# Two wide projections in the retention stage, with small elementwise work moved from GpSimd to ScalarE and VectorE

## The reference, cut to what matters

```python
def odd_mixer(xn, pos, w_in, ...):
    h = jnp.einsum('bsd,de->bse', xn, w_in)
    cx, dq, dk, dv, z = jnp.split(h, splits, axis=-1)
    oc = rglru_branch(cx, ...)              # stage C
    od = head_group_norm(retention_chunked(heads(dq), heads(dk), heads(dv), pos), ...)   # stage D
    y = jnp.concatenate([oc, od], axis=-1) * jax.nn.silu(z)
    return jnp.einsum('bse,ed->bsd', y, w_out)
# in rglru_branch, with xf the convolved input:
    r, ig = sigmoid(xb @ wa + ba), sigmoid(xb @ wx + bx)
    log_a = -RG_C * r * softplus(-lam)
    a = exp(log_a); u = sqrt(-expm1(2.0 * log_a)) * ig * xf
    h = scan(h_t = a_t * h_{t-1} + u_t)
# in retention_chunked: rotary(q), rotary(k) over the whole head, masked scores, values
```

## Time and profile before

| what | value |
| --- | --- |
| median of 3 runs | 579.88 us (579.59 to 580.05) |
| the profiled execution | 579.21 us, of which 577.5 us from the first to the last instruction |
| mean granted TensorE clock | 0.997 of 2.4 GHz |
| busy: PE | 569.6 us (99%) |
| busy: DVE | 440.1 us (76%) |
| busy: ACT | 398.5 us (69%) |
| busy: POOL | 67.8 us (12%) |

### The profile page before, as it was taken

How to read it: one execution, slowest core, us unless ns; L and a number is a source line. 1 busy time by engine, 2 the same in 40 slices (tenths; PEclk the granted TensorE clock), 3 DMA queues, 4 the chain that set the end, 5 groups by cost and what they waited for, 6 DMA issues and landing times.

```text
span 577.5 us, 8748 instructions
## 1 busy us (share of the span) xinstructions
PE 569.6 (99%) x3312; PEld 501.1 (87%) x3312; DVE 440.1 (76%) x696; ACT 398.5 (69%) x612; POOL 67.8 (12%) x76
## 2 busy tenths in 40 slices
PE   8999999999999999999999999999999999999995
PEld 7898889888888888888888889999899988888984
DVE  7888599698848874568768886799998974876763
ACT  7677794686657575647767858979669738466764
POOL 4002006039001000100000001111110100100002
PEclk9999999999999999999999999999999999999998
DMA  8757456457943544564346455326444564356202
GB/s 292 233 179 228 157 166 205 161 163 202 288 151 115 177 146 147 201 225 156 146 146 194 171 185 209 119 87 247 177 145 147 201 233 134 106 204 231 96 1 74
DMA packets 53134, 98.83 MB, mean 171 GB/s; under 512 B 1860, under 2 KB 8548, under 8 KB 53092
## 3 DMA queue, kind: packets, MB, share of 16 engines
q1 hardware_dynamic: 51908, 96.95, 49.9%
q0 software_dynamic: 1024, 1.05, 0.8%
q10 hardware_dynamic: 160, 0.27, 0.1%
HBM read 96.16 MB, written 1.05 MB: 168 GB/s over the span
## 4 chain that ended last, share of the span: by engine, by line
PE 97%; DMA 1%; DVE 1%; ACT 0%; issue 0%; DVEq 0%; SPq 0%; ACTq 0%
PE proj L2111 20%; PE proj L2112 10%; PE proj L2135 10%; PE proj L2137 10%; PE proj L2136 10%; PE proj L2094 5%; PE proj L2096 5%; PE proj L2095 5%; PE head L2341 4%; PE proj L2116 3%; PE proj L2115 1%; PE proj L2243 1%; PE head L2195 1%; DMA x_residual<-in_x_dram 1%; PE proj L2251 1%; PE head L2318 1%
## 5 line engine op out<-in xcount | busy, mean ns | idle before, releaser
L1258 DVE TENSOR_TENSOR w_lo<-raw_weights,w_hi 128x1024 fp32r<-128x1024 f32 x174 | 221.5, 1286 | 75.5 <-ACT w_hi L570 72.0
L570 ACT ACTIVATE w_hi<-raw_weights 128x1024 fp32r<-128x1024 f32 x174 | 181.9, 1056 | 99.6 <-PE proj L2137 48.2
L2111 PE MATMUL proj<-xT,w_hi 128*128 128x512 f32 x448 | 161.7, 400 | 0.0
L2112 PE MATMUL proj<-xT,w_lo 128*128 128x256 f32 x448 | 125.5, 280 | 0.0
L2111 PEld LDWEIGHTS proj<-xT,w_hi 128*128 128x128 f32 x448 | 84.3, 188 | 17.6
L2112 PEld LDWEIGHTS proj<-xT,w_lo 128*128 128x128 f32 x448 | 84.6, 189 | 2.0
L2094 PE MATMUL proj<-xT,w_hi 128*128 128x256 f32 x256 | 73.2, 286 | 0.0
L2095 PE MATMUL proj<-xT,w_hi 128*128 128x256 f32 x256 | 72.4, 283 | 0.0
L2096 PE MATMUL proj<-xT,w_lo 128*128 128x256 f32 x256 | 72.4, 283 | 0.0
L2135 PE MATMUL proj<-w_hi,y 128*128 128x512 f32 x176 | 69.2, 393 | 0.0
L2137 PE MATMUL proj<-w_lo,y 128*128 128x512 f32 x176 | 68.6, 390 | 0.0
(11 more groups left out here) (334 smaller groups left out, 937.7 us busy)
## 6 DMA issues: line engine op xcount, KB each, us to landing
raw_weights<-in_ev_w_in_dram SPq DMA_DIRECT2D x13, 2048.0 KB, 8.8
raw_weights<-in_od_w_in_dram SPq DMA_DIRECT2D x12, 2048.0 KB, 7.9
raw_weights<-in_ev_w_out_dram SPq DMA_DIRECT2D x4, 2048.0 KB, 7.9
raw_weights<-in_xa_wkv_dram SPq DMA_DIRECT2D x4, 2048.0 KB, 7.6
raw_weights<-in_od_w_out_dram SPq DMA_DIRECT2D x4, 2048.0 KB, 7.8
raw_weights<-in_xa_wq_dram SPq DMA_DIRECT2D x2, 2048.0 KB, 9.2
raw_weights<-in_xa_wo_dram SPq DMA_DIRECT2D x2, 2048.0 KB, 7.9
raw_weights<-in_ev_w_in_dram SPq DMA_DIRECT2D x6, 512.0 KB, 7.6
```

The lines of the kernel that those rows point to most:

```text
L570: act.activation(ring_quarter(w_hi, n, q), raw_quarter(n, q), ACT.Copy).then_inc(hi_ready, 1)
L1258: dve.tensor_tensor(ring_quarter(w_lo, n, q), raw_quarter(n, q), ring_quarter(w_hi, n, q).bitcast(F32), ALU.subtract).then_inc(lo_ready, 1)
L2111: pe.matmul(both, wh[:, k, :], x[:, :, k, :], start=(k == 0), stop=False)
L2112: pe.matmul(dst[:, 0:S], wl[:, k, :], x[:, 0, k, :], start=False, stop=False)
```

## The change

The q and k slabs of stage D group 0 become kind "X". Each half then needs a copy (ScalarE, `half_copied`) and a sum (VectorE, `half_summed`), after which the pair is free; the swap and the rotation read the sum in SBUF in place of PSUM. Both decay squares and `conv_high` go from GpSimd to ScalarE. The low part of the first gated scan goes from stage D group 0 to group 1 on VectorE, and one `y_low` goes from GpSimd to VectorE.

```diff
-    SLABS += [("D", "q", "F", _g), ("D", "k", "F", _g), ("D", "v", "T", _g), ("D", "z", "X", _g)]
+    SLABS += [("D", "q", "XF"[_g], _g), ("D", "k", "XF"[_g], _g), ("D", "v", "T", _g), ("D", "z", "X", _g)]
@@ gpsimd
-            decay_square(0)
             gated_input(1)
-            conv_high()
-            decay_square(1)
-            for i in range(5, 8):
-                y_low(i)
+            y_low(5)
+            y_low(7)
@@ scalar
             def tanhs(g):
...
-                last.then_inc(decay_ready, 1)
+                act.drain().then_inc(decay_ready, 1)
+            def decay_square(g):
+                act.wait_ge(input_gated, g + 1)
+                act.activation(conv_out(g), blocks(5), ACT.Square).then_inc(a_squared, 1)
+            def conv_high():
+                act.wait_ge(y_ready, 5)
+                act.activation(y_hi[:, 0:4, :], y_src(4), ACT.Copy).then_inc(conv_hi_ready, 1)
@@ scalar, stage_c: after z_half(z, 0)
                 if g:
+                    decay_square(0)
                     root_c(0)
+            def half_copied(n, w, u):
+                if n in D_WIDE:
+                    filled(act, n, 1, u)
+                    act.activation(blocks(w)[:, 2 * u:2 * u + 2, :], bank_halves(n, u, 0), ACT.Copy).then_inc(d_copied, 1)
@@ scalar, swap_halves: wide slabs wait for d_summed and read blocks(w)
@@ scalar, stage_d
+                half_copied(q, 0, 0)
                 ahead(q, 2)
-                swap_halves(q, 0)
+                swap_halves(q, 0, 0)
                 ahead(q, 3)
+                half_copied(q, 0, 1)
                 ahead(k, 0)
-                swap_halves(q, 1)
+                swap_halves(q, 0, 1)
...
                 if g == 0:
                     decays(1)
+                half_copied(k, 1, 0)
                 ahead(k, 2)
...
+                else:
+                    decay_square(1)
+                half_copied(k, 1, 1)
                 ahead(v, 0)
...
                 ahead(z, 0)
+                if g == 0:
+                    conv_high()
@@ vector
+            def gated_low(i):
+                G = i % 4
+                dve.wait_ge(y_hi_ready, i + 2)
+                dve.wait_ge(y_lo_ready, i + 2)
+                dve.tensor_tensor(y_lo[:, 4 * G:4 * G + 4, :], y_src(i), y_hi[:, 4 * G:4 * G + 4, :].bitcast(F32),
+                                  ALU.subtract).then_inc(y_lo_ready, 1)
+            def half_summed(n, w, u):
+                if n in D_WIDE:
+                    dve.wait_ge(d_copied, 2 * D_WIDE.index(n) + u + 1)
+                    rows = blocks(w)[:, 2 * u:2 * u + 2, :]
+                    dve.tensor_tensor(rows, bank_halves(n, u, 1), rows, ALU.add).then_inc(d_summed, 1)
+                    halves_freed(n, u)
@@ vector, stage_d
                 ahead(q, 0)
                 sum_z(slab("D", "z", 0) if g else slab("C", "z", 1), 1)
+                if g:
+                    dve.wait_ge(conv_hi_ready, 1)
+                    dve.tensor_tensor(y_lo[:, 0:4, :], y_src(4), ...)      # stood behind rope_full(q, 0) for g == 0
                 ahead(q, 1)
                 if g:
+                    dve.drain()
                     gated_d(0)
+                half_summed(q, 0, 0)
                 ahead(q, 2)
                 rope_full(q, 0, 0, q_ready, 4 * g + 1)
+                half_summed(q, 0, 1)
                 ahead(q, 3)
                 ahead(k, 0)
+                if g:
+                    gated_low(6)
                 ahead(k, 1)
+                half_summed(k, 1, 0)
                 rope_full(q, 1, 0, q_ready, 4 * g + 2)
...
                     one_minus_a2(1)
+                half_summed(k, 1, 1)
                 ahead(v, 0)
@@ tensor, stage_d: slab_x in place of slab_f for the wide slabs
```

More of the change, by code:

```diff
@@ L68 @@
 Z_SLABS = [n for n, s in enumerate(SLABS) if s[1] == "z"]
+D_WIDE = [n for n, s in enumerate(SLABS) if s[0] == "D" and s[1] in "qk" and s[2] == "X"]
 def slab(stage, part, g=0):
@@ L169, in hybrid_trunk @@
         a_squared = sem("a_squared")
+        input_gated = sem("input_gated")
         mem_landed = sem("mem_landed")
@@ L275, in hybrid_trunk @@
         halves_swapped = sem("halves_swapped")
+        d_copied = sem("d_half_copied")
+        d_summed = sem("d_summed")
         early_ms = sem("early_ms")
@@ L503, in gated_input @@
                 pool.wait_ge(igate_ready, g + 1)
[L504 to L515, removed]
+                pool.tensor_tensor(blocks(4), blocks(4), conv_out(g), ALU.mult).then_inc(input_gated, 1)
             def mem_placed(t):
@@ L1061, in tanhs @@
                 for h in range(4):
-                    last = act.activation(blocks(3)[:, h, :], blocks(3)[:, h, :], ACT.Tanh,
-                                          scale=soft[:, 6, 4 * g + h:4 * g + h + 1])
-                last.then_inc(decay_ready, 1)
+                    act.activation(blocks(3)[:, h, :], blocks(3)[:, h, :], ACT.Tanh,
+                                   scale=soft[:, 6, 4 * g + h:4 * g + h + 1])
+                act.drain().then_inc(decay_ready, 1)
[5 more added lines that the diff above has]
+                act.activation(y_hi[:, 0:4, :], y_src(4), ACT.Copy).then_inc(conv_hi_ready, 1)
             def root_c(g):
@@ L1140, in rstd_d, with swap_halves @@
                 act.activation(wview(4), wview(4), ACT.Exp, scale=-0.5).then_inc(o_rstd, 1)
-            def swap_halves(n, u):
-                filled(act, n, u)
+            def half_copied(n, w, u):
+                if n in D_WIDE:
+                    filled(act, n, 1, u)
+                    act.activation(blocks(w)[:, 2 * u:2 * u + 2, :], bank_halves(n, u, 0), ACT.Copy).then_inc(d_copied, 1)
+            def swap_halves(n, w, u):
+                wide = n in D_WIDE
+                if wide:
+                    act.wait_ge(d_summed, 2 * D_WIDE.index(n) + u + 1)
+                else:
+                    filled(act, n, u)
                 for a, b in ((0, 64), (64, 0)):
-                    last = act.activation(rope_tmp[a:a + 64, 2 * u:2 * u + 2, :],
-                                          bank(n, u)[b:b + 64, :].rearrange("p (h t) -> p h t", h=2), ACT.Copy)
+                    src = (blocks(w)[b:b + 64, 2 * u:2 * u + 2, :] if wide else
+                           bank(n, u)[b:b + 64, :].rearrange("p (h t) -> p h t", h=2))
+                    last = act.activation(rope_tmp[a:a + 64, 2 * u:2 * u + 2, :], src, ACT.Copy)
                 last.then_inc(halves_swapped, 1)
@@ L1172, in stage_d @@
                     decays(1)
+                half_copied(k, 1, 0)
                 ahead(k, 2)
                 act.wait_ge(q_ready, 2 + 2 * g + 1)
-                swap_halves(k, 0)
+                swap_halves(k, 1, 0)
                 if g == 0:
@@ L1181, in stage_d @@
                     dm(1, 1)
+                else:
+                    decay_square(1)
+                half_copied(k, 1, 1)
                 ahead(v, 0)
                 act.wait_ge(q_ready, 2 + 2 * g + 2)
-                swap_halves(k, 1)
+                swap_halves(k, 1, 1)
                 ahead(v, 1)
@@ L1936, in stage_c @@
                     gated_c(0)
+            def gated_low(i):
[10 more added lines that the diff above has]
+                    halves_freed(n, u)
             def rope_full(n, u, w, done, i):
+                wide = n in D_WIDE
                 dve.wait_ge(halves_swapped, i)
-                src = bank(n, u)[:].rearrange("p (h t) -> p h t", h=2)
                 dst = blocks(w)[:, 2 * u:2 * u + 2, :]
+                src = dst if wide else bank(n, u)[:].rearrange("p (h t) -> p h t", h=2)
                 tmp = rope_tmp[:, 2 * u:2 * u + 2, :]
@@ L1945, in rope_full @@
                 dve.tensor_tensor(tmp, tmp, trig[:, 1:2, :].broadcast_to([P, 2, S]), ALU.mult)
-                dve.drain().then_inc(free_of(n, u), 1)
+                if wide:
+                    dve.drain()
+                else:
+                    dve.drain().then_inc(free_of(n, u), 1)
                 dve.tensor_tensor(dst, dst, tmp, ALU.add).then_inc(done, 1)
@@ L1987, in stage_d @@
                 sum_z(slab("D", "z", 0) if g else slab("C", "z", 1), 1)
-                ahead(q, 1)
                 if g:
[L1990 to L1993, removed]
                     dve.wait_ge(conv_hi_ready, 1)
@@ L1996, in stage_d @@
                                       ).then_inc(y_lo_ready, 1)
+                ahead(q, 1)
+                if g:
+                    dve.drain()
+                    gated_d(0)
+                half_summed(q, 0, 0)
+                ahead(q, 2)
+                rope_full(q, 0, 0, q_ready, 4 * g + 1)
+                half_summed(q, 0, 1)
                 ahead(q, 3)
                 ahead(k, 0)
+                if g:
+                    gated_low(6)
                 ahead(k, 1)
+                half_summed(k, 1, 0)
                 rope_full(q, 1, 0, q_ready, 4 * g + 2)
@@ L2565, in stage_d @@
                 q, k, v, z = (slab("D", c, g) for c in "qkvz")
-                slab_f(q, [0])
```

(6 more changed lines are left out.)

## The result

The changed kernel takes 581.15 us (median of 9 runs, 580.54 to 583.25) against 579.52 us of the kernel before, measured beside it (9 runs): 1.0029 times, 95% interval 1.0018 to 1.0040. That is 1.6 us slower, more than the 0.2% that counted as no change, though the lower end of the interval (0.18%) lies just inside it. The range of 579.0 to 581.9 holds the time. The forecast of 580.5 is 0.65 us short of it, and the forecast change of +0.64 us is 1.0 us short of the measured one: the kernel before, too, was faster here (579.52) than ahead of the prediction (579.88). The profiled execution has a span of 579.0 us against 577.5, which is 1.5 us more. One of the nine runs took 583.25 us at a mean granted clock of 0.995, the others 580.54 to 581.51 at 0.996 to 0.999; the profile is of another run, so what happened in that one was not seen.

A forecast was written before the change was run, and what follows sets the result against it. TensorE was taken as the bound, busy 569.6 of 577.5 us. Terms -0.48 - 0.23 + 1.30 + 0.05 = +0.64 us took the median from 579.88 to 580.5 us, range 579.0 to 581.9.

The forecast's parts named there:

- a sign of being wrong: Start of stage D group 1 or its mean square: a TensorE wait over 0.3 us would show the prediction wrong.
- the rival on the square: First group's `one_minus_a2`: ScalarE's square ends after 375.61 and holds VectorE's chain; 581.1 to 581.9 us, chance 0.12.
- TensorE's own work, -0.48: Eight q and k quarters, stage D group 0: one 512-column matmul for two of 256 saves 0.06 us each, 0.48 us.
- The wait at q's start, -0.23: Start of q, stage D group 0: VectorE's earlier chain removes TensorE's wait at 380.08, gaining 0.23 us.
- VectorE 1.4 us earlier: Stage C convolution: without GpSimd's first square, two VectorE steps take 0.73 us, not 2.13; the chain moves up 1.40 us.
- The third quarter, +1.30: Third quarter of q: TensorE waits 1.20 us for the pair freed by VectorE's second z sum, plus 0.1 us behind it.
- Stage D group 1, nothing: Stage D group 1: 2 x 1.22 us more on VectorE, but TensorE's weights keep over 1 us of slack; no effect.
- the handshakes in stage D group 0: Copies and sums between ScalarE and VectorE make VectorE 2.06 us late at the second gated scan; 0.05 us counted for TensorE.
- a dead heat at group 1: Start of stage D group 1: bank pair free at 431.16, TensorE there at 431.15; 0.05 us counted.
- The third rival: Stage D group 0: VectorE half a microsecond later at each of k's two handshakes, 1 us stall; +1.6, 581.5 us, chance 0.15.
- two dead heats of 0.1 us or less: Group 1's start (pair 431.16, TensorE 431.15) and mean square a quarter later (VectorE about 433.9, TensorE 434.0).

The follow-up runs named there:

- the wide slabs alone: Kernel before with only q and k of stage D group 0 made kind X, squares, high part and low parts left in place: 584.86 us, ratio 1.0093.
- the early sum: Second half of stage C group 1's z slab copied and summed ahead of the gated scan; on the wide slabs alone: 585.20 us, ratio 1.0105.

## Why the prediction was right or wrong

*The place and the way* were right. TensorE's waits are at the two points that the text named, on VectorE's drains, and nowhere else in that stretch; the sign of the sum was right. But the text had put down a wait of over 0.3 us at the start of group 1 as a sign of being wrong, and one of 0.9 us came; and by its own 0.2% the outcome is slower, to which it gave 0.24, against 0.69 for the same. That the range holds the time is partly luck: its upper end came from the rival on the square, which fell, while the forecast's own range, 580.1 to 581.0, ends below 581.15. These terms were right:

- *TensorE's own work, -0.48.* From 386.93 to 403.96 six wide quarters take 17.03 us, 2.84 each with the slower step behind the wait (386.93 to 387.27, 0.34 us where the stream has 0.23) and 2.82 without it, as forecast. The weight loads of a quarter fall by a third, from 24 to 16, and not by half. The 2.60 us that the prediction worked out from the Trainium skill (TensorE: Matmul & The Clock Gate, Back-to-back issue gap) is not borne out here; that section gives the formula for an isolated matmul, and not for a stream of weight loads and matmuls such as this one.
- *The wait at q's start, -0.23.* The distance from the gates is 0.32 us shorter, but the first step of q takes 0.42 us (379.84 to 380.26) where the stream has 0.23, and that is 0.19 us lost where 0.10 was lost before: 0.23 us gained in all. The prediction took the slower step for the price of a wait; here it comes without one.
- *VectorE 1.4 us earlier.* The steps take 0.73 us; the z sum that frees the pair is at 386.15, where 386.01 was forecast and the trace after runs 0.1 us later from stage C on. The square ends at 374.89, where 374.9 was forecast, and no table load precedes it, so that rival fell.
- *The third quarter, +1.30.* It begins 1.33 us late, and the step behind it takes 0.11 us more: 1.44 us.
- *Stage D group 1, nothing.* From its first matmul to the end of the span it is 579.0 - 432.01 = 146.99 us, and it was 577.5 - 430.56 = 146.94; the 0.1 us of the step behind the wait are in that.

*The step that failed* is "the handshakes in stage D group 0", by its size. The text had a dead heat at group 1 and counted 0.05 us; measured are 0.70 us and the slower step behind it, 0.8 in all. VectorE's second gated scan was put at 423.26 and is at 424.13, its z sum at 430.37 and is at 431.23. Of this lateness 0.73 us are there by the sum of k's first half: it waits for a copy on ScalarE that the replay had ending at 400.35, and starts at 401.08. The rest comes behind it. Ahead of that copy the two engines wait for each other, and the trace shows small prices that the replay took too low. A half sum with its two releases holds VectorE from 394.41 to 395.32, 0.91 us where I took 0.78. The sum at the end of the first rotation starts 0.43 us after the product ahead of it has ended, against 0.08 in the later rotations. A swap from SBUF takes 1.28 us and not 1.20. How the 0.73 us divide among these stays open, as no run changed one of them alone.

The third rival, VectorE falling further behind, named this term and its price (each further microsecond costs one): +1.6 us, which is what was measured. It had a chance of 0.15, too low for a forecast that rested on two dead heats of 0.1 us or less. Where two queues arrive together, lateness counts and earliness doesn't, so the mean of the error is a loss; I should have priced the term at half a microsecond.

What the prediction did not see is that the first wait was not a price by itself. By the runs, without the 1.5 us wait the time stays the same: the chain through ScalarE's exps, the half sums and the second scan would have stopped TensorE at v and at group 1 instead. Adding the two waits gives the right total for the changed kernel (-0.48 - 0.23 + 1.44 + 0.8 = 1.5 us), and would have given a wrong one for its repair.

## What to carry to other kernels

Before saving work on the bound engine, ask for the order of the engines that feed it: here 0.5 us of TensorE time was bought with eight handshakes, and the kernel was slower until their order was mended, after which it was level. When a wait on the bound engine is removed, look up whether the operation which it waited for is on a chain that would stop it further on; the test is to move that operation, as was done here, and see whether new waits come that add up to as much. In a chain that goes to and fro between two engines, the handshake goes first and the independent work behind it: the one edit that broke this cost 1.0 us. Where the engine would stand idle for the other one, independent work goes into the gap, as the rotation of q did.

## What the runs showed of the hardware

The granted clock fell behind the long waits and not behind the shorter one. In the wide slabs alone, TensorE's weight loads waited 2.53 us before 388.54, and then the clock was 0.50 (1.2 GHz) up to 391.7 (columns: stretch, length, PE busy and matmuls, PEclk, DMA share, GB/s):

```profile
385.90:388.50 2.60, 0.43 (x3) 0.96 0.00 0
388.50:391.70 3.20, 3.16 (x10) 0.50 0.87 257
391.70:395.40 3.70, 3.70 (x23) 1.00 0.90 344
```

In that stretch a pair of matmuls takes 0.64 us in place of 0.35. In the changed kernel, behind 1.50 us of waiting (to 386.93), it stays at 1.00 (columns here: PE, PEld, DVE, ACT and POOL busy, then PEclk):

```profile
387.00:390.00 3.00, 3.00 (x17) 2.62 (x18) 2.66 (x2) 2.99 (x5) 1.46 (x1) 1.00 0.85 268
```

With the early sum the wide slabs alone wait 2.20 us in front of a quarter of v (to 412.91), and the clock falls there (columns as in the first of these tables):

```profile
413.00:416.50 3.50, 3.50 (x9) 0.55 0.00 0
```

The fall hardly shows in the time. The four runs of the wide slabs alone had mean clocks of 0.994, 0.994, 0.998 and 0.999 and took 585.04, 584.84, 584.89 and 584.71 us. My reading, which no run tests by itself, is that TensorE was slow in time that it would have waited through: behind the slow stretch it still waits 1.4 us at v and 1.2 us at group 1 for the chain on the other engines. That the clock fell at that place in the first two and not in the others was not seen, since one run alone is profiled.
